# An encoder block with expert FFN: SwiGLU, last router, row transposes and weighted sums put in another order

## The reference, cut to what matters

```python
h = rms_norm(x, norm_mix);  proj = h @ w_in                   # 1024 tokens, D = 1024
y_conv = short_conv_mixer(x_in, b_g, c_g, conv_w) @ w_out_conv
q, k = rms_norm(q), rms_norm(k)                               # 8 heads x 64
y_attn = neighbourhood_attention(q, k, v, rpb) @ w_out_attn   # 8 x 16 windows on a 16 x 64 grid
x = x + (sigmoid(gate_a) * y_conv + sigmoid(gate_b) * y_attn) @ w_o
h = rms_norm(x, norm_ffn)
logits = h @ w_router + b_router;  top 4 of 32 experts, gates = softmax(top values)
# for each expert e, on the rows that chose it:
g = minimum(xb @ w_gate[e] + b_gate[e], 7);  u = clip(xb @ w_up[e] + b_up[e], -7, 7)
act = g * sigmoid(1.702 * g) * (u + 1)                        # SwiGLU
x[rows] += (act @ w_down[e] + b_down[e]) * gate
```

## Time and profile before

| | before |
|---|---|
| runs, median (lowest, highest) | 2392.82 us (2389.49, 2395.52) |
| profiled execution, its own time | 2391.13 us |
| its span, first to last instruction | 2389.2 us |
| TensorE busy | 2303.7 us, 96% |
| VectorE busy | 1448.5 us, 61% |
| ScalarE, GpSimd busy | 1040.0 us, 907.3 us |
| chain that ended last | PE 82%, DVE 8%, issue 5% |
| mean granted clock of TensorE | 0.987 |
| moved by DMA | 505 MB |

### The profile page before, as it was taken

How to read it: one execution, slowest core, us unless ns; L and a number is a source line. 1 busy time by engine, 2 the same in 40 slices (tenths; PEclk the granted TensorE clock), 3 DMA queues, 4 the chain that set the end, 5 groups by cost and what they waited for, 6 DMA issues and landing times.

```text
span 2389.2 us, 34753 instructions
## 1 busy us (share of the span) xinstructions
PE 2303.7 (96%) x11110; PEld 1475.8 (62%) x11111; DVE 1448.5 (61%) x1855; ACT 1040.0 (44%) x1037; POOL 907.3 (38%) x495
## 2 busy tenths in 40 slices
PE   8999999999999968999999999999999999999996
PEld 4444444566665536777666666666676666666775
DVE  3123333411112357888877777777788777787895
ACT  2112322311110124666645565556466555565664
POOL 1123111000000013676654445644574564365563
PEclk9999999999999978999999999999999999999998
DMA  5412110022112246999887888898899888888995
GB/s 199 112 27 79 44 32 21 27 53 53 27 62 112 95 166 227 350 338 353 295 273 265 311 285 271 297 328 287 270 326 315 270 300 290 281 290 300 322 336 173
DMA packets 180337, 505.34 MB, mean 212 GB/s; under 512 B 18304, under 2 KB 60800, under 8 KB 180288
## 3 DMA queue, kind: packets, MB, share of 16 engines
q1 hardware_dynamic: 164160, 457.99, 53.6%
q0 software_dynamic: 16128, 46.67, 9.1%
HBM read 468.36 MB, written 32.05 MB: 209 GB/s over the span
## 4 chain that ended last, share of the span: by engine, by line
PE 82%; DVE 8%; issue 5%; DVEq 2%; DMA 2%; ACT 1%; POOL 0%; SPq 0%; ACTq 0%; POOLq 0%
PE psum L1531 13%; PE psum L1533 11%; PE psum L1532 11%; PE psum L1380 7%; PE psum L1324 7%; PE psum L1412 4%; PE psum L1475 4%; PE psum L1542 4%; DVE w_lo L1120 3%; PE psum L1424 2%; PE psum L1423 2%; PE psum L1422 2%; PE psum L1584 2%; PE psum L1560 1%; PE psum L1342 1%
## 5 line engine op out<-in xcount | busy, mean ns | idle before, releaser
L1120 DVE TENSOR_TENSOR w_lo<-ring,w_hi 128x2048 fp32r<-128x2048 f32 x384 | 874.4, 2307 | 68.7 <-ACT w_hi L751 58.9
L751 ACT ACTIVATE w_hi<-ring 128x2048 fp32r<-128x2048 f32 x384 | 723.6, 1919 | 166.1 <-DMA ring<-in_w_down 95.9
L592 POOL TENSOR_SCALAR pick<-iota_bf,slot_col 128x256 bf16<-128x256 bf16 x252 | 509.0, 2032 | 56.4 <-DVE slot_col L1133 56.4
L1531 PE MATMUL psum<-w_hi,xT_hi 128*128 128x512 f32 x992 | 411.5, 415 | 28.4 <-DVE w_lo L1120 26.9
L1533 PE MATMUL psum<-w_hi,xT_lo 128*128 128x512 f32 x992 | 394.3, 397 | 0.0
L1532 PE MATMUL psum<-w_lo,xT_hi 128*128 128x512 f32 x992 | 393.9, 397 | 0.0
L598 POOL DMA_INDIRECT xg<-h_rows,idx_new x33 | 70.0, 2120 | 573.5 <-DVE idx_new L1114 556.3
L1531 PEld LDWEIGHTS psum<-w_hi,xT_hi 128*128 128x128 f32 x992 | 187.2, 189 | 150.3 <-issue 56.7
L1531 PE MATMUL psum<-w_hi,aT_hi 128*128 128x512 f32 x544 | 228.2, 419 | 8.6 <-issue 4.0
L1533 PE MATMUL psum<-w_hi,aT_lo 128*128 128x512 f32 x544 | 216.9, 399 | 0.0
L1532 PE MATMUL psum<-w_lo,aT_hi 128*128 128x512 f32 x544 | 216.1, 397 | 0.0
(11 more groups left out here) (259 smaller groups left out, 2896.1 us busy)
## 6 DMA issues: line engine op xcount, KB each, us to landing
ring<-in_w_gate SPq DMA_DIRECT2D x256, 512.0 KB, 5.0
ring<-in_w_up SPq DMA_DIRECT2D x256, 512.0 KB, 6.4
ring<-in_w_down SPq DMA_DIRECT2D x256, 512.0 KB, 5.5
ring<-in_w_in SPq DMA_DIRECT2D x28, 512.0 KB, 5.2
ring<-in_x SPq DMA_DIRECT2D x16, 512.0 KB, 3.2
ring<-in_w_in SPq DMA_DIRECT2D x6, 1024.0 KB, 7.4
vb<-oT SPq DMA_DIRECT2D x16, 256.0 KB, 9.2
ring<-in_w_o SPq DMA_DIRECT2D x4, 1024.0 KB, 5.9
```

The source lines that it names most:

```text
L592: e.tensor_scalar(pick[:, t, :], iota_bf[:, :], slot_col[:, t, :], None, ALU.is_equal).then_inc(g_pick, 1)
L751: e.activation(w_hi[:, hs, :], ring[:, slot, :], ACT.Copy).then_inc(g_hi, 1)
L1120: e.tensor_tensor(w_lo[:, hs, :], ring[:, slot, :], w_hi[:, hs, :].bitcast(F32), ALU.subtract).then_inc(g_lo, 1)
L1531: e.matmul(dst, hi, w_up, start=start, stop=False)
```

## The change

Nothing is computed in another way. Four things change place.

1. In the loop VectorE's `swiglu` goes from behind the second remainder of a round to behind `xT_lo` of the round before; the first one stands ahead of the loop, with `evacuate(0)` directly before it.
2. In the attention `weighted` goes behind `scores` of two pairs later, and the convolution's steps of a pair are one piece; `attn_out` follows.
3. In the passage the last `router` stands before the positions of the tile before it, and VectorE's `top` and `routed` of that tile go ahead of the last scaled rows; the logits are a step of their own; `gates_of(TT - 4)` goes behind `first_numbers`; GpSimd builds three of the first picks and VectorE four.
4. `rows_transpose(0)` stands before `pass_rows`, `rows_transpose(1)` behind the seventh chunk of the first pass in place of the eighth, and ScalarE's roundings around them change places.

```diff
@@ -576,7 +576,7 @@
...
             e.wait_ge(f_slot, 1)
-            for t in range(4):
+            for t in range(3):
                 e.tensor_scalar(pick[:, t, :], iota_bf[:, :], slot_col[:, t, :], None, ALU.is_equal).then_inc(g_pick, 1)
...
@@ -779,15 +779,16 @@
...
                 e.activation(ys[:, 512:D], bank[5][:, :], ACT.Copy, scale=gate_cur[:, 0:1]).then_inc(g_y, 1)
-            for k in range(SPLIT - 1):
+            for k in range(MSLOT):
                 round_weights(0, k, True)
             round_rows(0, aT_hi, aTb, 4, 7)
-            round_weights(0, SPLIT - 1, True)
+            for k in range(MSLOT, SPLIT):
+                round_weights(0, k, True)
             e.activation(warm[:, :], half[:, 0:1], ACT.Sigmoid)
...
                 round_weights(0, k, False)
+            round_weights(0, 8, False)
             round_rows(1, xT_hi, xTb, 4, 7)
-            round_weights(0, 8, False)
             e.wait_ge(table_ok, 1)
...
@@ -976,10 +977,11 @@
...
                 normalise(n)
-                if n:
-                    attn_out(n - 1)
+                if n >= 2:
+                    attn_out(n - 2)
                 conv_products((conv_at[n] + 3) // KT, conv_at[n + 1] // KT)
                 one_tap(taps_ready(conv_at[n + 1]))
+            attn_out(pairs - 2)
             attn_out(pairs - 1)
...
@@ -1021,11 +1023,13 @@
...
 
-            def top(t):
+            def logits_out(t):
                 e.wait_ge(e_lg, t + 1)
...
                                        op0=ALU.mult, op1=ALU.add).then_inc(e_lc, 1)
+
+            def top(t):
                 e.wait_ge(e_lc, t + 1)
...
@@ -1063,9 +1067,13 @@
...
                 if t == TT - 1:
+                    logits_out(t - 1)
                     h2_evac(t)
...
                 e.tensor_scalar(var[:, t:t + 1], ss[:, t:t + 1], 1.0 / D, EPS, ALU.mult, ALU.add).then_inc(e_var, 1)
+                if t == TT - 1:
+                    top(t - 1)
+                    routed(t - 1)
                 e.wait_ge(e_rs, t + 1)
...
@@ -1073,20 +1081,21 @@
...
                                        op0=ALU.mult, op1=ALU.mult).then_inc(e_xn, 1)
-                if t:
+                if 0 < t < TT - 1:
+                    logits_out(t - 1)
                     top(t - 1)
...
                     gates_of(t - 3)
-            gates_of(TT - 4)
             e.wait_ge(f_pe, 1)
...
             e.tensor_tensor(slot_col[:, 0:TT - 1, 0], pos[:, 0:TT - 1, 0], rt[:, 0:TT - 1, 0], ALU.mult).then_inc(f_slot, 1)
-            e.wait_ge(f_slot, 1)
-            for t in range(4, TT - 1):
-                e.tensor_scalar(pick[:, t, :], iota_bf[:, :], slot_col[:, t, :], None, ALU.is_equal).then_inc(g_pick, 1)
+            logits_out(TT - 1)
             top(TT - 1)
             routed(TT - 1)
+            e.wait_ge(f_slot, 1)
+            for t in range(3, TT - 1):
+                e.tensor_scalar(pick[:, t, :], iota_bf[:, :], slot_col[:, t, :], None, ALU.is_equal).then_inc(g_pick, 1)
             e.wait_ge(f_pe, 2)
...
@@ -1192,6 +1201,7 @@
...
             first_numbers()
+            gates_of(TT - 4)
             gates_of(TT - 2)
...
@@ -1248,16 +1258,15 @@
...
             hb0 = e.value_load(table[0:1, NT:NT + 1], min_val=0, max_val=1)
-            evacuate(0, hb0)
             rest_of_rows(1, xT_hi, xT_lo, 4)
             rest_of_weights(0, 8)
+            evacuate(0, hb0)
+            swiglu(0, hb0)
             row_numbers(2, 7)
             with e.Fori(0, n_loop) as p:
-                hb = e.value_load(table[0:1, bass.ds(p + NT, 1)], min_val=0, max_val=1)
                 hbn = e.value_load(table[0:1, bass.ds(p + (NT + 1), 1)], min_val=0, max_val=1)
...
                 rest_of_weights(p, 8 + 1)
-                swiglu(p, hb)
                 for k in range(2, 4):
...
@@ -1272,11 +1281,11 @@
...
                 rest_of_rows(p + 2, xT_hi, xT_lo, 0)
+                swiglu(p + 1, hbn)
                 shift_rows(p, False)
...
             hbe = e.value_load(table[0:1, bass.ds(n_loop + NT, 1)], min_val=0, max_val=1)
-            swiglu(n_loop, hbe)
             rest_of_weights(n_loop, 8 + 1)
...
@@ -1385,11 +1394,11 @@
...
                 scores(n)
-                conv_steps(conv_at[n], conv_at[n] + 3)
-                if n:
-                    weighted(n - 1)
-                conv_steps(conv_at[n] + 3, conv_at[n + 1])
+                if n >= 2:
+                    weighted(n - 2)
+                conv_steps(conv_at[n], conv_at[n + 1])
                 prob_transpose(n)
+            weighted(pairs - 2)
 
...
@@ -1482,8 +1491,8 @@
...
             h2_transpose(TT - 1)
+            router(TT - 1)
             positions(TT - 2)
-            router(TT - 1)
             last_positions()
...
@@ -1604,8 +1613,8 @@
...
             def first_gate_up(b):
+                rows_transpose(0, 4, 7)
                 pass_rows()
-                rows_transpose(0, 4, 7)
                 e.wait_ge(g_copy, 1)
...
@@ -1613,7 +1622,8 @@
...
                         slot_rows(1, ex1, 7)
-                rows_transpose(1, 4, 7)
+                    if k == 6:
+                        rows_transpose(1, 4, 7)
                 gate_up_bias(0, b)
...
```

## The result

The changed kernel takes 2430.92 us (median of 4 runs, 2427.63 to 2432.31); the kernel before took 2393.58 beside it (2389.49 to 2395.52). The ratio is 1.0161, with a 95% interval of 1.0149 to 1.0173: slower by 1.6%. The profiled execution has a span of 2425.7 us, 36.5 more than before, and a mean granted clock of 0.978 (before 0.987). TensorE is busy for 95% of it.

A forecast was written before the change was run, and what follows sets the result against it. TensorE, busy 96% of the span, was taken to bound the kernel, so only its waits and idle time count. 2391.1 + 32.3 + 19 - 2.4 - 8.3 - 0.8 = 2430.9, predicted as 2430 us, range 2404 to 2442.

The forecast's parts named there:

- Loop waits: Loop: SwiGLU delays the first chunk's remainder at 30 boundaries; 53.0 us of new waits replace 20.7, so +32.3.
- The rival of the covered place: Loop: VectorE reaches SwiGLU 2.7 us sooner, the 20.7 us of waits go and nothing returns: 2359 us; chance 0.12.
- The rival of the transfers: Loop: transfers set the short passes, so eight plain boundaries with plain SwiGLU add nothing: 2408 us; chance 0.08.
- Clock: Loop: 12 of 15 new waits of 2.7 to 3.3 us drop TensorE to half clock: +19 us.
- The price: Loop: each fall of TensorE's clock costs 1.6 us, read from nine slow matmul starts behind a 2.02 us wait.
- Attention: Attention: sums directly behind scores and convolution in one piece save 3 us, less 0.6: -2.4.
- what a piece stands behind is worth 0.1 us, and one of four such borders a pair goes: Attention: removing one border between convolution and small products saves 0.1 us a pair, -3 us, bounds 0 to -6.
- The 0.6 taken off for later exponentials: Attention: exponentials and normalising come about 0.80 us later, costing 0.6 us in the few pairs with little room.
- Passage: Passage: earlier table, first product and second pass bring the loop's start forward by 8.3 us; bounds -3 to -11.
- The sign given for the first product: Passage: the first pass's first product, at 898.67 before, was to come near 892.6 us.
- partly lost: Passage, second pass: SwiGLU before the second chunk's remainder takes 1 to 3 us, so 8.3 of 9 remain.
- Tail: Tail: the 3.3 us wait for `ut` goes, but VectorE has the same work before `aT_lo`: -0.8, 0 to -3.3.

The follow-up runs named there:

- a_swiglu_back: The changed kernel with SwiGLU back between the second and third gate/up remainders, all else as changed: 2380.73 us, ratio 0.9952 to the kernel before.
- b_swiglu_moved: The kernel before with SwiGLU alone moved to its changed place: 2441.61 us, ratio 1.0208.
- fourth: The changed kernel with SwiGLU in the loop behind the fourth gate/up chunk's remainder: 2359.32 us, ratio 0.9867 to the kernel before.
- third_long: The changed kernel with SwiGLU back between second and third remainders and an extra VectorE instruction ahead of it: 2415.28 us, ratio 1.0098 to the kernel before.
- fourth_evac: The changed kernel with SwiGLU behind the fourth remainder and the first pass's evacuation back ahead of the rows' and ninth chunk's remainders: 2358.32 us.
- p_router: The kernel before with the router's part of the passage edits alone: 2389.87 us, ratio 0.9994.
- b_passage: The kernel before with all passage edits alone, attention and SwiGLU as before: 2386.68 us, ratio 0.9974.
- ut_ahead: The changed kernel with SwiGLU's first product between the last two down remainders, the second at the changed place: 2387.33 us, ratio 0.9982 to the kernel before.
- six more: The changed kernel with SwiGLU put back, and five of the kernel before with attention or passage edits alone, whole or part: ratios 0.9952 to 0.9994.

## Why the prediction was right

The direction and the mechanism were right. That the time, 2430, was right within 1 us is partly luck: the attention gave 3.6 us more than predicted, the loop lost 4.2 less and the passage gained 4.1 less, and of the 39.8 us of the sum the spans show 36.5. The profiled execution is also the fastest of the changed kernel's four, 3.3 us under their median.

**Loop waits, predicted 53.0, measured 52.7.** The 30 boundaries are as counted: 8 of 2.68 to 2.90 (predicted 2.71), 7 of 3.24 (3.26), 8 of 0.73 (0.82), 7 of 0.18 to 0.20 (0.27); the third chunk waits nowhere. Reading the slack of the first remainder, 0.06 us in the earlier trace rows and 1.27 in the earlier trace rows, gave the whole term. a_swiglu_back and b_swiglu_moved show the move to be the whole loss. The rival of the covered place is out; fourth's 2359 is the value that it gave, by a place that is covered, two down and not one up. The rival of the transfers is out for this change too: all eight plain boundaries with the short SwiGLU lengthened.

**Clock, predicted 19, measured 15.** The loop's 47.1 less 32.0 of waits leaves 15.1. The count, 12 of 15, was right by luck: b_swiglu_moved has 13, and the reason given, that most of the waits are nearer to 3.5 than to 2.0 us, does not hold, since the 8 of 2.71 are nearer to 2.0. Only the 7 of 3.26 are nearer to 3.5, and at those seven the clock fell each time. The price was the mis-sized term: 1.6 us from the earlier trace rows belongs to the third chunk, where third_long shows 1.7; at the first chunk a fall costs 0.9, and one of about 7 us some 2 (57.2 us for a pass, where those like it with a single fall take 56.0 to 56.1). 9 x 0.9 + 3 x 2 = 14.1, less the 1.6 of the old fall, is 12.5; the other 2.6 would be what 13 added waits cost beyond their recorded length, an estimate: without a fall the pass from 2350.28 took 41.6 us with a wait of 2.69, and fourth_evac's at 2242.34, with none, 38.7, so 0.2 each.

**Attention, predicted -2.4, measured -6.0 and, alone, -6.5 by the medians.** The step that failed is "what a piece stands behind is worth 0.1 us, and one of four such borders a pair goes". 0.1 is the difference between two kinds of border; the one that goes is worth 0.20, 30 times. The 0.6 taken off for later exponentials was not there, TensorE waits nowhere in the attention. The value lay at the end of the bounds that I gave.

**Passage, predicted -8.3, measured -4.2.** The table came 1.2 us sooner (p_router; predicted 1) and the first product 5.4 sooner than the attention accounts for (predicted 6). The second pass's first chunk came forward 8.2 (14.2 less 6.0; predicted 9). (The sign given for the first product, 892.6, left the attention's gain out; it is at 887.28.) The step that failed is that SwiGLU would take 1 to 3 us "partly lost" there and the loop inherit 8.3. The wait became 5.75 us, and SwiGLU is 2.1 of the loss: without it moved, the stretch is 6.5 shorter than before, not 8.3. The other 1.8 is not settled. The evacuation's new place, with its wait of 2.03 for `gt`, suggests itself, but fourth_evac put it back and gained nothing that can be told. The passage's sum has no term for the clock, which in the changed kernel is low for 3.5 us more there than before and in a_swiglu_back for about as long (6.9 us) as before. Nor do attention and passage simply add up: b_passage, with the attention as before, gains 4.7 us there, not 6.5.

**Tail, predicted -0.8, measured -0.4.** Waits of 3.3 and 3.5 us became one of 6.15 for `aT_lo`.

## What to carry to other kernels

Before an instruction is moved ahead of others on an in-order engine, read the slack of the first thing queued behind its new place: here 0.06 us, and all of the 2.7 us showed. Look in both directions and ask when the result is needed; behind the fourth remainder SwiGLU is covered, and that place gave 21 us over the old one. When edits come in a bundle, time the parts by themselves: here one edit lost 50 us, and the rest of the bundle was good for 11.

## What the runs showed of the hardware

- Whether TensorE's clock falls at a wait is no matter of its length alone: it fell at 6 of 15 waits of 1.1 to 1.6 us at the boundary of a pass (ut_ahead), and at none of 84 of 1.0 to 1.7 us at the third chunk, inside a run of full products (the kernel before, third_long and six more). The Trainium skill (TensorE: Matmul & The Clock Gate, on how the oscillation bites in real kernels) describes the clock falling again in every tile of a kernel that waits in each; here three of fifteen boundaries with the longest waits kept it. Why the place counts stays open; ahead of the boundary stand a bias product and small products, but no run varied these.
- The Trainium skill (TensorEngine Tiling (Array Packing), Key Properties) says that changing the tiling mode drains the engine, with no price. The runs agree in sign and give one that hangs on what stands ahead. A border is 0.20 us for a full product behind scores, 0.11 behind weighted sums, and weighted sums behind scores none that shows (scores take 0.85 us to the next row in either order).
- GpSimd's `pick` takes 2032 ns on the mean before and 1593 in the changed kernel, 2013 and 1591 with SwiGLU alone put back or moved. Nothing of GpSimd's was changed in the last; only VectorE's order was. The median is 0.91 us in all of them and the longest about 5 us, so the mean is made by the long ones. These instructions are off the path here; what slows them wasn't tried.
